# A decoder trunk's prologue rebuilt: half of x first, the activations rounded from the transposes, small loads put off, and one mean-square product a norm

## The chip, the cores and the metric

The kernel runs on one core of a Trainium2 chip. The metric is the device time of one execution in microseconds (us): 1108.33 us is the median of three runs of the kernel before (1108.31 to 1109.08). Five engines work beside each other, each with an instruction stream of its own: TensorE (PE in the rows, with its weight loads PEld), VectorE (DVE), ScalarE (ACT), GpSimd (POOL) and SyncE (SP), which here only issues transfers. They wait for each other on semaphores.

## The reference

A trunk of two layers on x, 256 tokens by 1024 channels, float32. Each layer is

```
x = x + 0.5 * swiglu(rmsnorm(x, g1), w_gate, w_up, w_down)        # width 2816
h = rmsnorm(x, g_mix)
q, k, v, c_b, c_c, c_u, g_attn, g_conv = split(h @ w_in)          # 5120 columns
y_attn = rmsnorm(diff_attention(q, k, v, rel_bias, lam)) @ w_branch_attn
y_conv = (c_b * causal_conv3(c_c * c_u)) @ w_branch_conv
x = x + (sigmoid(g_attn) * y_attn + sigmoid(g_conv) * y_conv) @ w_out
x = x + 0.5 * swiglu(rmsnorm(x, g2), ...)
```

with `rmsnorm(x, g) = x * rsqrt(mean(x*x) + eps) * g`, and `lam = exp(sum(lq1*lk1)) - exp(sum(lq2*lk2)) + const`, one number a layer. The relative-position bias of the attention is a table of 32 buckets by 4 heads, spread over the distances. A last rmsnorm follows.

## The kernel before

**Tiling.** Activations stand transposed, channels on the 128 partitions: `xt` holds x as 8 tiles of 128 channels by 256 tokens. Weights stream in units of 512 KB, 4 tiles of 128 rows by 256 columns (`raw`, a ring of 4 slots). To keep float32 accuracy with the faster rounded format, each operand is split into a rounded part (hi) and the rest (lo). ACT rounds a weight unit (`hi()`, line 474), DVE subtracts it to get the rest (`lo()`, line 755), and PE forms for each of the 4 tiles two products of the hi weights with the 512 columns of hi and lo activations (line 1109) and two of the lo weights with the 256 hi columns (line 1118). One such unit is 16 matmuls. The activations `xm` are split in the same way: gain times x (`xg`), rounded by ACT, subtracted by DVE, in pairs of tiles (`xm_lo` counts finished pairs).

**Units and sets.** Two units with the same 256 output columns make a set, which ends in one of two accumulators `acc`. ACT copies half of it out (`copy_acc`, line 486), DVE adds the other half (`sum_acc`, line 767); only then can PE begin the next set there. In the first two sets behind a norm the units are taken in turn: set 0 first half of x, set 1 first half, set 0 second half, set 1 second half. I number them units 0, 1, 2, 3; later sets take their two units in a row. A gate set and an up set make one pair of tiles of the feed-forward hidden layer (`gate_up`): DVE scales the gate sum by `rstd`, ACT takes Silu, DVE multiplies by the up sum, ACT rounds (line 543), DVE subtracts (line 852). In `gate_up(1)` the units are 7 to 10, `gate_up(2)` begins with unit 11.

**Order within an engine.** Every stream is written out by hand. A weight transfer is issued when the unit four before it has been split by DVE (`lo_split`). ACT's `hi` of a unit waits for the transfer and for PE's end with the unit four before. DVE's `lo` waits for `hi`. PE's `multiply` (line 1098) waits for both before its first matmul.

**The norm.** The mean square over channels is a product with a matrix of 1/1024 (`mean_square`, line 1146): two float32 matmuls over the two halves of `square_sum`. PE does it between units 1 and 2. `norm_start` on DVE (line 800) clears `square_sum` and adds eps, `norm_root` on ACT (line 501) takes the reciprocal root, `norm_rstd` on DVE refines it in three steps. The norm happens six times, and a seventh form at the end uses tokens as columns.

**The prologue.** SP issues both halves of x, then the four first weight units (lines 351 to 358). ACT issues the first norm's gain as a strided load, the bias table and the one-hot `places`. PE turns x by 16 transposes into the accumulators (line 1182). ACT copies them to `xt` (line 565), DVE multiplies by the gain (line 888), ACT rounds (line 572), DVE subtracts (line 903). In between PE spreads the bias table by 8 matmuls (line 1190), ACT copies the four results (line 583). ACT squares x (line 578), DVE sums the squares (line 910). Then ACT sums the lambda products, takes Exp and loads the Silu table again (lines 586 to 597). POOL loads the lambda rows (line 409), multiplies them, issues 14 loads of small parameters (line 419), and sends the bias rows through DRAM and back (lines 431 to 437). PE waits for all four pairs of `xt` before unit 0.

Of the kernel before, what the change touches and what calls it, by code (L numbers as in the profile page):

```python
# [31 lines left out]
P = 128  # L32
# [19 lines left out]
PAIR = 2  # L52
# [3 lines left out]
LEAD = 3  # L56
ACCS = 2
# [41 lines left out]
def bucket_places():  # L99
# [8 lines left out]
    return places  # L108
# [47 lines left out]
def trunk(nc, x, norm_ffn1_g, ffn1_w_gate, ffn1_w_up, ffn1_w_down, norm_mix_g, w_in,  # L156
# [3 lines left out]
    with ExitStack() as ctx:  # L160
# [6 lines left out]
        def sem(name):  # L167
# [28 lines left out]
        square_sum = sb("square_sum", [PAIR, SEQ])  # L196
        mean_sq = sb("mean_sq", [SEQ])
# [28 lines left out]
        first_g = sb("first_g", [KT])  # L226
        eps = sb("eps", [1])
        table_probe = sb("table_probe", [1 + 3 * DEPTH])
# [9 lines left out]
        table_hi = hm[:, 0, :].rearrange("p (h m) -> p h m", h=N_HEADS)  # L238
        table_lo = hm[:, 1, :].rearrange("p (h m) -> p h m", h=N_HEADS)
# [16 lines left out]
        out_msq_ps = acc[0][:, 0, 0:QT]  # L256

# [14 lines left out]
            "x_new", "squared", "square_added", "xg_ready", "xm_hi", "xm_lo"))  # L272
        msq_summed, msq_ready, inv_ready = (sem(n) for n in ("msq_summed", "msq_ready", "inv_ready"))
# [15 lines left out]
            "x_turned", "lam_multiplied", "lam_summed", "lam_exped"))  # L289
        table_ready, bias_spread, bias_rows_ready = sem("table_ready"), sem("bias_spread"), sem("bias_rows_ready")  # L290
# [23 lines left out]
        def _(sp):  # L314
# [21 lines left out]
            def two_sets(l, wa, a, wb, b, in_turn=False):  # L336


                if not in_turn:
                    full(wa, l, a)  # L340
                    full(wb, l, b)
                    return
                for k in range(0, KT, UK):
                    load(rows(wa, l)[:, k:k + UK, bass.ds(a, COLS)])
                    load(rows(wb, l)[:, k:k + UK, bass.ds(b, COLS)])
# [5 lines left out]
            for b in range(2):  # L351
# [3 lines left out]

            for l in range(DEPTH):

                two_sets(l, ffn1_w_gate, 0, ffn1_w_up, 0, in_turn=True)
# [36 lines left out]
        def _(pool):  # L395

            nc.gpsimd.memset(ident[:, :], 0.0).then_inc(ident_zeroed, 1)
            nc.gpsimd.memset(mean_ones[:, :], 1.0 / D_MODEL).then_inc(ones_ready, 1)
# [5 lines left out]
            nc.gpsimd.memset(eps[:, :], SUBLN_EPS).then_inc(ones_ready, 1)  # L404


# [46 lines left out]
        def _(act):  # L453
# [57 lines left out]
            def two_sets(between=None):  # L511
# [3 lines left out]
                if between:  # L515
                    hi()
                    between()
                copy_acc(3 if between else 2)
# [5 lines left out]
            def ffn():  # L524
# [782 lines left out]
```

## Time and profile before

| | us |
|---|---|
| median of three runs | 1108.33 |
| lowest, highest | 1108.31, 1109.08 |
| the profiled execution's own time | 1108.66 |
| its span, first to last instruction | 1106.9 |
| PE busy (share of the span) | 1089.0 (98%) |
| PEld busy | 961.5 (87%) |
| DVE busy | 829.6 (75%) |
| ACT busy | 643.6 (58%) |
| POOL busy | 20.2 (2%) |
| mean traffic of the transfers | 182 GB/s |

The busy times are sums over one engine's instructions; engines overlap, so they do not add up. The outline of the span in 40 slices shows PE at 9 tenths or more in every slice but the first (7) and the last (6). A row of the chain of waits gives start, length and what ran; a row of the timeline gives start, time, engine, line, operation, and in brackets the idle time before it and what ended that.

### The profile page before, as it was taken

How to read it: one execution, taken by the hardware profiler on the slowest of the kernel's cores; microseconds unless marked ns; L12 is line 12 of the kernel's file. 1: busy time of each engine (PE TensorE's matmuls, PEld its weight loads, DVE VectorE, ACT ScalarE, POOL GpSimd, SP SyncE). 2: the span in 40 equal slices, each digit the busy share in tenths (PEclk: the TensorE clock that was granted, in tenths of full speed). 3: DMA queues.
4: the chain of work that ended last, by engine and by line, in shares of the span. 5: the costliest groups of instructions: out<-in, count | busy, mean ns of one | idle time of the engine just before them, and what ended most of it. 6: DMA issues, size and time to landing. Idle time of an engine off the chain costs nothing.

```text
span 1106.9 us, 19503 instructions
## 1 busy us (share of the span) xinstructions
PE 1089.0 (98%) x6512; PEld 961.5 (87%) x6512; DVE 829.6 (75%) x1016; ACT 643.6 (58%) x908; POOL 20.2 (2%) x38
## 2 busy tenths in 40 slices
PE   7999999999999999999999999999999999999996
PEld 6888888888899988888888888888888998888885
DVE  5876766778898877766787776767888988677666
ACT  7655644556775665654466565445767656565454
POOL 5100000000000000000000000000000000000000
PEclk9999999999999999999999999999999999999998
DMA  8856556655566566665566656566455656656561
GB/s 211 250 182 201 175 167 193 203 172 157 170 192 186 163 199 193 180 189 189 178 192 180 202 172 197 168 202 199 145 160 181 200 174 180 200 174 207 169 196 40
DMA packets 202451, 201.64 MB, mean 182 GB/s; under 512 B 7904, under 2 KB 201472, under 8 KB 202416
## 3 DMA queue, kind: packets, MB, share of 16 engines
q1 hardware_dynamic: 200288, 199.25, 58.8%
q0 software_dynamic: 992, 1.87, 0.9%
q8 instruction: 21, 0.34, 0.1%
q10 hardware_dynamic: 1136, 0.05, 0.1%
q14 instruction: 14, 0.11, 0.0%
HBM read 199.32 MB, written 1.84 MB: 182 GB/s over the span
## 4 chain that ended last, share of the span: by engine, by line
PE 97%; DMA 1%; ACT 1%; DVE 0%; issue 0%; SPq 0%; DVEq 0%; ACTq 0%
PE acc L1109 58%; PE acc L1118 31%; PE acc L1113 4%; DMA raw<-in_ffn_w_gate_dram 1%; PE mixed L1113 1%; PE score L1113 1%; PE score L1217 0%; PE mixed L1151 0%; PE mixed L1118 0%; PE score L1118 0%; PE mixed L1238 0%; PE mixed L1225 0%; PE mixed L1231 0%; ACT L508 0%; ACT w_hi L474 0%
## 5 line engine op out<-in xcount | busy, mean ns | idle before, releaser
L1109 PE MATMUL acc<-xm,w_hi 128*128 128x512 f32 x2048 | 648.0, 398 | 2.3 <-ACT xt L565 2.3
L755 DVE TENSOR_TENSOR w_lo<-raw,w_hi 128x1024 fp32r<-128x1024 f32 (+1 forms) x387 | 455.5, 1199 | 139.6 <-ACT w_hi L474 139.2
L1118 PEld LDWEIGHTS acc<-xm,w_lo 128*128 128x128 f32 x2048 | 385.9, 188 | 91.4
L474 ACT CAST w_hi<-raw 128x1024 fp32r<-128x1024 f32 (+1 forms) x387 | 390.5, 1033 | 121.3 <-PE acc L1118 109.6
L1118 PE MATMUL acc<-xm,w_lo 128*128 128x256 f32 x2048 | 403.5, 278 | 0.0
L1109 PEld LDWEIGHTS acc<-xm,w_hi 128*128 128x128 f32 x2048 | 313.4, 189 | 3.1 <-ACT xt L565 2.8
L1109 PE MATMUL acc<-hm,w_hi 128*128 128x512 f32 x704 | 221.1, 395 | 0.0
L1118 PEld LDWEIGHTS acc<-hm,w_lo 128*128 128x128 f32 x896 | 162.2, 189 | 31.3
L1118 PE MATMUL acc<-hm,w_lo 128*128 128x256 f32 x896 | 177.0, 279 | 0.0
L486 ACT COPY acc_lo<-acc 128x512 f32<-128x512 f32 x144 | 84.2, 585 | 128.6 <-PE acc L1118 128.2
L767 DVE TENSOR_TENSOR sum<-acc,acc_lo 128x512 f32<-128x512 f32 x144 | 99.1, 688 | 48.2 <-ACT acc_lo L486 47.4
L1109 PEld LDWEIGHTS acc<-hm,w_hi 128*128 128x128 f32 x704 | 107.2, 189 | 0.0
L543 ACT CAST hm<-ffn_store 128x512 f32 (+1 forms) x44 | 27.4, 622 | 74.2 <-DVE ffn_store L849 74.2
L1113 PE MATMUL acc<-hm,w_hi 128*128 128x256 f32 x384 | 61.7, 283 | 0.0
L852 DVE TENSOR_TENSOR hm<-ffn_store,hm 128x512 f32 (+1 forms) x44 | 30.5, 693 | 33.7 <-ACT hm L543 33.7
L1113 PEld LDWEIGHTS acc<-hm,w_hi 128*128 128x128 f32 x384 | 53.0, 192 | 0.0
L495 ACT ACTIVATE square<-xt 128x512 f32 (+1 forms) x24 | 15.2, 634 | 58.9 <-DVE xt L874 41.3
L536 ACT ACTIVATE ffn_store<-sum 128x512 f32<-128x512 f32 x44 | 27.9, 635 | 29.3 <-DVE sum L837 29.3
L849 DVE TENSOR_TENSOR ffn_store<-sum,ffn_store 128x512 f32<-128x512 f32 x44 | 30.5, 693 | 6.3 <-DVE sum L767 2.5
L837 DVE TENSOR_TENSOR sum<-sum,rstd 128x512 f32<-128x512 f32 x44 | 30.4, 692 | 1.4
L824 DVE TENSOR_TENSOR late<-sum,rstd 128x512 f32 (+1 forms) x28 | 19.4, 692 | 1.0
L945 DVE SCALAR_TENSOR_TENSOR ffn_store<-score,bias 128x768 f32<-128x768 f32 x8 | 7.7, 958 | 16.4 <-PE score L1219 16.4
(145 smaller groups left out, 463.1 us busy)
## 6 DMA issues: line engine op xcount, KB each, us to landing
raw<-in_ffn_w_gate_dram SPq DMA_DIRECT2D x88, 512.0 KB, 4.7
raw<-in_ffn_w_up_dram SPq DMA_DIRECT2D x88, 512.0 KB, 4.0
raw<-in_ffn_w_down_dram SPq DMA_DIRECT2D x80, 512.0 KB, 4.6
raw<-in_w_in_dram SPq DMA_DIRECT2D x80, 512.0 KB, 4.5
raw<-in_w_out_dram SPq DMA_DIRECT2D x16, 512.0 KB, 4.1
raw<-in_ffn_w_down_dram SPq DMA_DIRECT2D x16, 256.0 KB, 3.2
raw<-in_w_branch_attn_dram SPq DMA_DIRECT2D x8, 512.0 KB, 3.5
raw<-in_w_branch_conv_dram SPq DMA_DIRECT2D x8, 512.0 KB, 3.5
```

Of the source, the lines that this page charges most:

```text
L474: nc.scalar.copy(w_hi[:, s, 0:tiles, :], raw[:, s, 0:tiles, :]).then_inc(hi_split, 1)
L486: nc.scalar.copy(acc_lo[s][:, :, :], acc[s][:, :, SEQ:2 * SEQ]).then_inc(acc_copied, 1)
L536: nc.scalar.activation(silu[:, :, :], sums[0][:, :, :], ACT.Silu).then_inc(silu_done, 1)
L543: nc.scalar.copy(hm[:, at(i * PAIR), 0:SEQ], hid[:, :, :]).then_inc(hid_hi, 1)
L755: nc.vector.tensor_tensor(w_lo[:, s, 0:tiles, :], raw[:, s, 0:tiles, :], w_hi[:, s, 0:tiles, :], ALU.subtract).then_inc(lo_split, 1)
L767: nc.vector.tensor_tensor(sums[s][:, :, :], acc[s][:, :, 0:SEQ], acc_lo[s][:, :, :], ALU.add).then_inc(acc_summed, 1)
L837: nc.vector.tensor_tensor(gate, gate, wide(rstd[:, :]), ALU.mult).then_inc(gate_ready, 1)
L849: nc.vector.tensor_tensor(hid[:, :, :], up, silu[:, :, :], ALU.mult).then_inc(hid_ready, 1)
L852: nc.vector.tensor_tensor(h_at[:, :, SEQ:2 * SEQ], hid[:, :, :], h_at[:, :, 0:SEQ], ALU.subtract).then_inc(hid_lo, 1)
L1109: nc.tensor.matmul(banks[:, m, :], w_hi[:, r, k, cols], x[:, 0:2 * SEQ], start=first and k == 0, stop=False, skip_group_check=True)
L1113: nc.tensor.matmul(banks[:, m, 0:SEQ], w_hi[:, r, k, cols], x[:, at_x:at_x + SEQ], start=first and k == 0 and at_x == 0, stop=False, skip_ ...
L1118: mm = nc.tensor.matmul(banks[:, m, 0:SEQ], w_lo[:, r, k, cols], x[:, 0:SEQ], start=False, stop=last and k == ends, skip_group_check=True)
```

## The change

It does five things.

1. **Loads.** SP issues the first half of x, the first gate unit, then the second half of x, then the other units. The first gain is loaded as 8 rows of 128 instead of 1024 single values, and PE transposes it. `places` and the bias table are loaded twice, into 64 partitions. GpSimd's loads wait until the first pair of hidden tiles is rounded (`hid_hi`), and all of its later work stands behind them.
2. **PE.** Eight float32 matmuls of 128 by 128 on the constant matrix run ahead of everything. Only the first half of x is turned before unit 0; the second half is turned behind unit 0. The spreading of the bias table is 4 matmuls over 64 partitions. Unit 0 does all its hi products first and waits for the lo weights only then.
3. **Rounding.** ACT rounds gain times x straight out of the transposes in PSUM, one tile an instruction, and DVE subtracts straight from PSUM too. The copies to `xt` come last on ACT, behind the squares. ACT begins with the Silu table and waits for the small loads (`table_loaded`) before it rounds anything.
4. **Lambdas.** ACT's sums, the Exp and the return to Silu stand behind the second `gate_up` of the first layer.
5. **Norm.** DVE adds the two halves of `square_sum` (`join_squares`), PE does one mean-square matmul instead of two, and does it ahead of unit 3 instead of unit 2. `norm_start` stands behind `sum_acc`, and ACT's root behind `copy_acc`.

```diff
 # SP
-            for b in range(2):
+            def load_x(b):
                 half = slice(b * D_MODEL // 2, (b + 1) * D_MODEL // 2)
                 sp.dma_start(x_tok[:, :, half], ...).then_inc(x_loaded[b], 16)
+            load_x(0)
-                two_sets(l, ffn1_w_gate, 0, ffn1_w_up, 0, in_turn=True)
+                two_sets(l, ffn1_w_gate, 0, ffn1_w_up, 0, in_turn=True,
+                         after_first=None if l else lambda: load_x(1))
 # GpSimd
+            nc.gpsimd.memset(mean_ones[:, :], 1.0 / D_MODEL).then_inc(ones_ready, 1)
+            nc.gpsimd.memset(eps[:, :], SUBLN_EPS).then_inc(ones_ready, 1)
             nc.gpsimd.memset(ident[:, :], 0.0).then_inc(ident_zeroed, 1)
...
+            pool.wait_ge(hid_hi, 1)
             for n, v in enumerate((lambda_q1, lambda_k1, lambda_q2, lambda_k2)):
 # ScalarE
-            act.dma_start(first_g[:, :], columns(norm_ffn1_g[0]), allow_slow_non_contiguous=True) \
+            act.dma_start(gain_rows[0:KT, :], norm_ffn1_g[0].rearrange("(k p) -> k p", p=P)) \
                 .then_inc(gain_loaded, 16)
+            for n in range(2):
+                act.dma_start(table[n * NUM_BUCKETS:(n + 1) * NUM_BUCKETS, :], rel_bias).then_inc(table_loaded, 16)
+            act.dma_start(onehot[0:2 * NUM_BUCKETS, :], places).then_inc(table_loaded, 16)
+            act.wait_ge(ones_ready, 2)
+            have_table(ACT.Silu)
+            act.wait_ge(table_loaded, 48)
+            nc.scalar.copy(onehot_r[0:2 * NUM_BUCKETS, :], onehot[0:2 * NUM_BUCKETS, :]).then_inc(onehot_ready, 1)
+            def pairs_hi(first):
+                for p in (first, first + 1):
+                    act.wait_ge(x_turned, p + 1)
+                    for k in range(PAIR):
+                        last = nc.scalar.activation(xm[:, p * PAIR + k, 0:SEQ], side[p][:, k * SEQ:(k + 1) * SEQ],
+                                                    ACT.Copy, scale=first_g[:, p * PAIR + k:p * PAIR + k + 1])
+                    last.then_inc(xm_hi, 1)
+            act.wait_ge(gain_ready, 1)
+            pairs_hi(0)
+            hi()
             act.wait_ge(bias_spread, 1)
             for h in range(N_HEADS):
-                last = nc.scalar.copy(bias_rows[:, h, :], side[h][:, 0:BIAS_LEN])
+                last = nc.scalar.copy(bias_rows[:, h, :], spread[h][:, 0:BIAS_LEN])
             last.then_inc(bias_copied, 1)
+            hi()
+            pairs_hi(2)
+            hi()
+            for p in range(XPAIRS):
+                act.wait_ge(xm_lo, p + 1)
+                nc.scalar.activation(squares[p]..., side[p], ACT.Square).then_inc(squared, 1)
+            for p in range(XPAIRS):
+                nc.scalar.copy(xt[:, at(p * PAIR), :]..., side[p]).then_inc(x_new, 1)
...
+            def lambdas():
+                act.wait_ge(lam_multiplied, 1)
...
+                have_table(ACT.Silu)
 # ScalarE, gate_up in ffn
-                        norm_root()
-                    copy_acc(3 if first else 2)
+                        wait(act, (square_joined, norm.now + 1))
+                    copy_acc(3 if first else 2)
+                    if first:
+                        norm_root()
...
+                if after_second:
+                    gate_up(1, False)
+                    after_second()
 # VectorE
+            def join_squares():
+                wait(dve, (square_added, pair.now))
+                nc.vector.tensor_tensor(square_one[:, :], square_sum[:, 0, :], square_sum[:, 1, :],
+                                        ALU.add).then_inc(square_joined, 1)
...
                     if first:
-                        norm_start()
                         lo()
                     gate = sum_acc()
                     if first:
+                        norm_start()
                         norm_rstd()
...
+            def pairs_lo(first):
+                for p in (first, first + 1):
+                    dve.wait_ge(xm_hi, p + 1)
+                    for k in range(PAIR):
+                        last = nc.vector.scalar_tensor_tensor(out=xm[:, t, SEQ:2 * SEQ],
+                            in0=side[p][:, k * SEQ:(k + 1) * SEQ], scalar=first_g[:, t:t + 1],
+                            in1=xm[:, t, 0:SEQ].bitcast(F32), op0=ALU.mult, op1=ALU.subtract)
+                    last.then_inc(xm_lo, 1)
+            dve.wait_ge(gain_ready, 1)
+            pairs_lo(0)
+            lo()
+            lo()
+            pairs_lo(2)
+            lo()
 # TensorE
-                wait(pe, (square_added, pairs.now), (bias_copied, 1))
-                for m in range(PAIR):
-                    mm = nc.tensor.matmul(msq_ps, mean_ones[:, :], square_sum[:, m, :], ...)
+                wait(pe, (square_joined, norm.now + 1), (x_new, XPAIRS))
+                nc.tensor.matmul(msq_ps, mean_ones[:, :], square_one[:, :], start=True, stop=True)
...
-                    if between and (j, n) == (0, 1):
+                    if between and (j, n) == (1, 1):
                         between()
+                    if after_first and (j, n) == (0, 0):
+                        multiply_in_two(banks[j], [tiles[:, k, :] for k in range(UK)],
+                                        (made, count.now - UK // PAIR))
+                        after_first()
+                        continue
...
+            pe.wait_ge(ones_ready, 1)
+            for _ in range(WARM):                                        # WARM = 8
+                nc.tensor.matmul(warm_ps, mean_ones[:, :], mean_ones[:, :], start=True, stop=True)
             pe.wait_ge(ident_ready, 1)
+            pe.wait_ge(gain_loaded, 16)
+            nc.tensor.transpose(gain_ps, gain_rows[0:KT, :], ident[0:KT, 0:KT]).then_inc(gain_turned, 1)
+            def second_half():
+                pe.wait_ge(bias_copied, 1)
+                turn_pairs(2)
+            turn_pairs(0)
```

`multiply_in_two` is `multiply` with the 8 hi products first, then the wait for `lo_split`, then the 8 lo products. `turn_pairs` holds the 8 transposes of one half of x.

## Rows read from the trace of the kernel before

**Rows 1.** The page: the chain that ended last, shares of the span by engine

```profile
PE 97%; DMA 1%; ACT 1%; DVE 0%; issue 0%; SPq 0%; DVEq 0%; ACTq 0%
```

**Rows 2.** Chain of waits, first 50 us: start us, length us, what

```profile
1.75 9.97 DMA raw<-in_ffn_w_gate_dram
...
11.74 1.05 ACT w_hi L474
...
19.06 0.85 PE acc L1109 x2
...
21.22 0.46 PE acc L1109 x2
```

**Rows 3.** A window: us, busy us of PE, PEld, DVE, ACT, POOL, PEclk, DMA share, GB/s

```profile
0.00:20.30 20.30, 12.29 (x41) 10.24 (x42) 9.27 (x13) 12.30 (x21) 12.32 (x25) 1.00 0.80 199
```

**Rows 4.** Timeline of PE: start, us, engine, line, operation, count [idle before <-releaser]

```profile
4.91 1.94 PE L1182 MATMUL acc<-ident,late 128*128 128x128 f32 x8 [4.91 <-DMA late<-in_x_dram]
7.16 1.97 PE L1182 MATMUL acc<-ident,late 128*128 128x128 f32 x8 [0.30 <-DMA late<-in_x_dram]
9.64 1.65 PE L1190 MATMUL score<-hm 32*128 32x384 f32 x4 [0.51 <-DVE hm L899]
...
14.85 1.22 PE L1109 MATMUL acc<-xm,w_hi 128*128 128x512 f32 x2 [2.29 <-ACT xt L565]
...
26.84 0.63 PE L1109 MATMUL acc<-xm,w_hi 128*128 128x512 f32 x2
...
38.01 0.63 PE L1109 MATMUL acc<-xm,w_hi 128*128 128x512 f32 x2
```

**Rows 5.** Transfers of the first 12.5 us: issuer, count, KB, us to landing

```profile
part<-in_places_dram ACTq DMA_DIRECT2D x1, 48.0 KB, 6.5
first_g<-in_norm_ffn_g_dram ACTq DMA_DIRECT2D x1, 4.0 KB, 4.6
```

**Rows 6.** Timeline of ACT in the prologue

```profile
8.45 0.51 ACT L569 CAST hm<-part 32x384 fp32r<-32x384 f32 x1 [0.97 <-DMA part<-in_places_dram]
...
18.09 1.15 ACT L578 ACTIVATE acc_lo<-xt 128x512 f32<-128x512 f32 x2
19.14 0.83 ACT L583 COPY proj<-score 128x384 f32<-128x384 f32 x2
...
20.61 0.29 ACT L590 ACTIVATE lam_scratch<-lam_prod 128x64 f32<-128x64 f32 x1
...
21.95 1.28 ACT L508 ACT_TABLE_LOAD   x1
...
23.36 2.94 ACT L474 CAST w_hi<-raw 128x1024 fp32r<-128x1024 f32 x3
```

**Rows 7.** Timeline at the kernel's end: scaled copies out of PSUM, transposes

```profile
1093.87 1.04 PE L1273 MATMUL score<-ident,late 128*128 128x128 f32 x8
...
1101.14 1.57 ACT L725 ACTIVATE late<-score,out_rstd 128x256 f32<-128x256 f32 x4 [0.68 <-DVEq L1077]
```

**Rows 8.** Timeline of DVE: the lo parts of units 3 and 4

```profile
24.42 2.36 DVE L755 TENSOR_TENSOR w_lo<-raw,w_hi 128x1024 fp32r<-128x1024 f32 x2 [1.40 <-ACT w_hi L474]
```

**Rows 9.** Timeline of ACT: the hi parts of units 11 and 12

```profile
44.49 2.00 ACT L474 CAST w_hi<-raw 128x1024 fp32r<-128x1024 f32 x2
```

**Rows 10.** Timeline of POOL

```profile
11.41 0.87 POOL L414 TENSOR_TENSOR lam_prod<-lam_rows 128x128 f32<-128x128 f32 x2 [7.33 <-DMA lam_rows<-in_lambda_k_dram]
...
30.11 0.75 POOL L437 DMA_DIRECT2D bias<-bias_scratch  x1
```

**Rows 11.** Line 862 of DVE: count, duration min/median/max ns, first and last start

```profile
L862 DVE COPY cur<-pars x2: 176/178/179, 144.8 to 683.0; 128x38 f32<-128x38 f32 x2
```

**Rows 12.** Chain of waits at the second norm

```profile
208.17 0.86 PE mixed L1151 x4
```

**Rows 13.** Timeline at the third norm: ACT's hi of units 7, 8; PE's unit 7

```profile
387.19 2.00 ACT L474 CAST w_hi<-raw 128x1024 fp32r<-128x1024 f32 x2
...
391.35 0.63 PE L1109 MATMUL acc<-xm,w_hi 128*128 128x512 f32 x2
```

More of the change, by code:

```diff
@@ L594, in _ @@
[L594 to L599 removed]
+            hi()
+            pairs_hi(2)
+            hi()
+            squares = (square_sum, square, acc_lo[0], acc_lo[1])
+            for p in range(XPAIRS):
+                act.wait_ge(xm_lo, p + 1)
+                nc.scalar.activation(squares[p][:, :, :].rearrange("p k n -> p (k n)"), side[p],
+                                     ACT.Square).then_inc(squared, 1)
@@ new lines, in _ @@
+            for p in range(XPAIRS):
+                nc.scalar.copy(xt[:, at(p * PAIR), :].rearrange("p k n -> p (k n)"), side[p]).then_inc(x_new, 1)
+            pair.add(XPAIRS)
+            def lambdas():
+                act.wait_ge(lam_multiplied, 1)
+                for s in range(2):
+                    for l in range(DEPTH):
+                        n = s * DEPTH + l
+                        last = nc.scalar.activation(lam_scratch[:, s, l * HEAD_DIM:(l + 1) * HEAD_DIM],
+                                                    lam_prod[:, s, l * HEAD_DIM:(l + 1) * HEAD_DIM], ACT.Copy,
+                                                    accum_out=lam_sum[:, n:n + 1])
+                last.then_inc(lam_summed, 1)
+                act.wait_ge(lam_summed, 1)
+                nc.scalar.activation(lam_exp[:, :, :], lam_sum[:, :].rearrange("p (s l) -> p s l", s=2),
+                                     ACT.Exp).then_inc(lam_exped, 1)
+                have_table(ACT.Silu)
@@ L600, in _ @@
+            for l in range(DEPTH):
+                ffn(None if l else lambdas)
                 two_sets(norm_root)
@@ L882, in _ @@
             dve.sem_inc(square_added, 1)
[L884 to L900 removed]
+            dve.sem_inc(xg_ready, XPAIRS)
@@ L1096, in _, with multiply_in_two @@
             slot = [0]
+            def multiply_in_two(banks, x_tiles, *needs):
+                r = slot[0] % RING
+                wait(pe, *needs, (hi_split, unit.now + 1))
+                for k, x in enumerate(x_tiles):
+                    for m in range(PAIR):
+                        nc.tensor.matmul(banks[:, m, :], w_hi[:, r, k, m * P:(m + 1) * P], x[:, 0:2 * SEQ],
+                                         start=k == 0, stop=False, skip_group_check=True)
+                wait(pe, (lo_split, unit.now + 1 + RING))
+                for k, x in enumerate(x_tiles):
+                    for m in range(PAIR):
+                        mm = nc.tensor.matmul(banks[:, m, 0:SEQ], w_lo[:, r, k, m * P:(m + 1) * P], x[:, 0:SEQ],
+                                              start=False, stop=False, skip_group_check=True)
+                mm.then_inc(used, 1)
+                unit.add()
+                slot[0] += 1
             def multiply(banks, x_tiles, first, last, *needs, halves=True):
```

146 lines of the change are left out of this document (59 added, 87 removed).

## The prediction

> **What bounds the kernel now.** I read the page's chain first: 97% of it is PE [rows 1]. So the time is PE's work plus what keeps PE from starting. Then the chain of the first 50 us in order of time: the first gate unit's transfer lands at 11.72 us, ACT rounds it, and the first real matmul starts at 14.85 us [rows 2, 4]. PE waited 4.91 us for x and 2.29 us just ahead of unit 0 [rows 4]. From then on I find no hole in PE: unit 3 starts at 26.84 and unit 7 at 38.01, which makes (38.01 - 26.84) / 4 = 2.79 us a unit [rows 4]. Last the pace: a pair of hi matmuls takes 0.85 us at 19.06 and 0.46 at 21.22 [rows 2]. The granted clock of the window up to 20.3 us reads 1.00 [rows 3], so it misses this; by the pace I take the engine to have run at 1.2 GHz until about 20.3 us and at 2.4 GHz after, though it had turned x and spread the bias table between 4.91 and 12.6 [rows 4].
>
> Two prices follow. A us by which PE's steady run starts earlier is a us of the result, if PE never waits afterwards. And whatever leaves PE's steady stream counts in full. I work out when units 3 and 11 start, where the before has 26.84 and 26.84 + 8 x 2.79 = 49.14.
>
> **When ACT can start.** ACT now rounds nothing before `table_loaded`. The `places` load took 6.5 us from issue to landing, behind the strided gain on the same queue (4.6 us) [rows 5]; ACT found it at 8.45 [rows 6]. It becomes the fourth issue, at about 2.45 us (0.73 + 3 x 0.55, an estimate from the issues' spacing), and twice as large. What goes is the 1024 single values ahead of it and POOL's lambda loads. Bounds: 4.6 us to landing gives 7.05, 6.5 gives 8.95; below, landing stops mattering where the first transposes are done, 4.91 + 1.94 / 2 = 5.9. I take 7.0, the nearest row being the gain's. The gate unit is now second in SP's queue, where the second half of x (same 512 KB) had landed by 7.16 [rows 4], and ACT wants it at 8.95. So that load is hidden. If it still landed at 11.72, all below moves by 2.8.
>
> **ACT up to unit 0.** One-hot copy 0.45 (0.51, ends overlap) [rows 6]; four scaled copies of 256 columns from PSUM, by 1.57 for four at the end of the kernel [rows 7], 1.5; hi(0) 0.98 (2.94 / 3) [rows 6]. 7.0 + 0.45 + 1.5 + 0.98 = 9.95. DVE's share (four fused subtractions, then lo(0)) runs beside it; the split form of unit 0 needs lo(0) only 8 matmuls later. The four spreading matmuls took 1.65 us [rows 4] and fit between 8.1 and 9.8. PE starts unit 0 at 10.0, 4.85 us before the old start.
>
> **The clock.** This is where I must choose. Before, 2.9 us of spreading matmuls and a hole of 2.29 us did not bring the fast level; 5.5 us of unit 0 without a hole did. Now 8 warm-up matmuls of two passes each run from about 1.0 to 4.9 us (16 x 0.24, by the transposes' 1.94 / 8 [rows 4]), then transposes and a wait, then the spreading, a hole of 0.2 to 0.4 us, and unit 0. Bounds: fast from the first matmul, or slow through unit 0 (5.1 us) and, with the transposes interrupting, through unit 1. I take fast from 13.0, some 3 us into unit 0, between the two. Then the hi half of unit 0 ends at 13.25, the lo half (8 x 0.12) at 14.2, four transposes at 0.13 each [rows 7] at 14.7.
>
> **ACT up to unit 3.** The bias copies (1.47 for four, 19.14 to 20.61 [rows 6]) and hi(1) are done by 12.5, hidden under unit 0, and `bias_copied` is there in time. From 14.75: four scaled copies 1.5, hi(2) 1.0, four squares 2.1 (18.09 to 19.14 for two [rows 6]), four copies to `xt` 2.1 (taken as the squares), hi(3) 1.0: 22.45. DVE's lo(3) adds 1.25 [rows 8]: 23.7. PE meanwhile turns the rest of x (done 15.25), runs units 1 and 2 (to about 20.9) and then waits; the mean square, which now needs all of `x_new`, falls into that wait and costs nothing here. So PE holds a hole of some 2.3 us before unit 3. Unit 3 starts at 23.7, which is 3.1 us earlier than before.
>
> **ACT up to unit 11: the lambdas.** Until `gate_up(2)` the chain of ACT and DVE, not PE, sets the pace, as it did before: from hi(3)'s end (23.36 + 0.98 = 24.34) to the end of the second rounding of hidden tiles, where hi(11) starts (44.49), it took 20.15 us [rows 6, 9]. The root now stands behind `copy_acc` and `norm_start` behind `sum_acc`, which I price at 0.5 (0.8 for the two DVE instructions less what waited anyway; bounds 0 and 1.0): 20.65. Then the lambdas. The four sums with Exp took 20.61 to 21.95, 1.34 us, and the Silu table 1.28 [rows 6]. Exp now needs a table of its own, 1.28 more: 3.9 us. Add hi(11) 1.0 and lo(11) 1.25. 22.45 + 20.65 + 3.9 + 2.25 = 49.25. PE would be there at 23.7 + 0.7 (small waits at units 4 and 7) + 8 x 2.79 = 46.7. So PE waits some 2.5 us, and unit 11 starts at 49.25, 0.1 us later than before. The prologue's lead is given back.
>
> ACT must not wait for the lambda rows on top. `hid_hi` comes at about 33.4; the four issues take 2.4 us; before, the product stood ready 7.33 + 0.87 us behind the last issue [rows 10]: 33.4 + 2.4 + 8.2 = 44.0, and ACT arrives at 43.1. In that stretch there is less other traffic, so I take 0, with 0.9 as the bound above by this row.
>
> Later, ACT catches up within one `gate_up`: unit 15 is wanted 11.2 us after unit 11, and a turn of the ACT and DVE chain takes 9.7. POOL's rest (small parameters, bias through DRAM) took 30.86 - 11.41 = 19.5 us [rows 10] and ends near 64, the wait for them on DVE stands at 144.8 [rows 11]. Their traffic beside the weights was there before, at 12 to 36 us, and no weight unit was late.
>
> **The later norms.** One mean square costs PE 0.86 us for the four passes of two matmuls [rows 12]. Half goes: 0.43 in each of the five later norms, 2.15. The root comes later against PE by the one set that it now stands behind. Before, hi(7) began 4.16 us ahead of unit 7 [rows 13] and needs 1.0 + 1.25 with some 0.7 lost to hi(8) and other work between; I reckon hi(7) later by 0.5 and PE earlier by 0.4, which leaves about 1 us. Cost 0, bound 0.4 each. The join is 0.4 us of DVE (estimate, half a 512-column add of 0.69); it lies under units 0 to 2, and at the end under PE's last mean square; bound 0.4 there.
>
> **Sum.** +0.1 (unit 11) - 2.15 = -2.05 us. The profiled execution's own time is 1108.66 for a span of 1106.9; it lies 0.33 above the median. 1106.9 - 2.05 = 1104.85, with 1.76 around it 1106.6, and by the median 1108.33 - 2.05 = 1106.3. I say 1106.3.
>
> **A rule against it.** The table loads follow each other here without a pause: 21.95 + 1.28 = 23.23, and hi(3) starts at 23.36 after the probe [rows 6]. The Trainium skill, ScalarE: Activation LUTs, section What ACT_TABLE_LOAD costs, says that a switch of table costs about 2.66 us, 1.28 for the load and 1.38 of drain. By that rule the two switches of the lambdas would cost 2.8 us more than I count, and the sum would be about 1109.0. The rows show no such drain.
>
> **The rivals.** Everything behind unit 0 hangs on one chain, so a shift of unit 3 is a shift of the result.
>
> *Forecast*, unit 3 near 23.7: 1106.3, own range 1105.3 to 1107.3. Chance 0.40.
>
> *The clock is fast from unit 0 on*: unit 0 takes 2.8, x is turned at 13.3 instead of 14.7, unit 3 starts at 22.3: 1104.9. For it: the warm-ups last 3.9 us and the spreading follows. Against it: the pause between them holds only transposes and waiting, and in the rows transposes with spreading did not do it. An early landing of `places` (5.9) would give up to 1.1 more. Chance 0.26.
>
> *The clock is slow through unit 1*: unit 0 5.1, four transposes 1.0, unit 1 5.1, unit 2 ends at 25.0, mean square, unit 3 at 25.5: 1108.1. Chance 0.10.
>
> *`places` lands late*, at 9.0: the chain moves by 2.0, 1108.3. Chance 0.07.
>
> *The order of loads does nothing*, the gate unit lands at 11.7 still: +2.8, 1109.1. Against it: SP's queue was served in order for x. Chance 0.06.
>
> *The tables drain*, as in the rule above: 1109.1. Chance 0.04.
>
> *Slower: ACT stands at the lambda rows.* ACT's queue is in order; behind the wait stand all hi parts, behind these lo and PE. The rows are fetched through POOL only once `hid_hi` is up, beside the weight stream. Each us by which the product comes after 43.1 is a us of PE idle. It turns the result to a loss from a product at 45.2 (2.05 us late), and beyond the 0.2% from 47.4, that is 11.6 us behind the last issue against the row's 8.2. At 15 us behind it the product comes at 50.8, 7.7 after ACT: 1106.3 + 7.7 = 1114.0. Against it: the row of 7.33 was taken with the transfers at their fullest. Chance 0.07.
>
> **How the numbers follow.** A measurement here tells about 0.2%, 2.2 us, from no change: faster is below 1106.1, slower above 1110.5. Faster: 0.21 of the forecast's 0.40 and all of 0.26, 0.47. Slower: 0.07. Same: 0.46. The range takes the fast clock with part of the early landing (1104.0) and on the other side the late starts (1109.0); it leaves out the slow rival and the tails of the others.
>
> **What would show it.** After: `table_loaded` met near 7.0, first line-1109-like matmul (in the split unit) near 10.0; the pair of hi matmuls falling from 0.85 to 0.46 within unit 0; a PE wait near 2 us before unit 3, released by DVE's lo; a second one near 2.5 us before unit 11, behind an ACT_TABLE_LOAD for Exp; half as many mean-square passes, 12 instead of 24, each saving 0.43; no PE wait at the later norms. The prediction is wrong in its main step if PE shows no wait at unit 11, and then the result is up to 2.5 us better.

## The result, and the profile after

The changed kernel takes 1110.33 us, the median of 17 runs (1108.93 to 1110.82), against 1108.40 for 17 runs of the kernel before beside them (1107.65 to 1109.39). The ratio is 1.0015, with the 95% interval 1.0008 to 1.0021: slower by some 2 us where 2 us less were forecast, above the range's 1109.0. The profiled execution took 1110.61 us for a span of 1108.7; before, it was 1108.66 for 1106.9. So the trace has 1.8 us to explain, and 3.9 against the forecast.

I read it in the order of the prediction. First the page's chain, the row that answers to [rows 1]:

```profile
PE 94%; DVE 2%; ACT 2%; issue 1%; DMA 1%; ACTq 0%; DVEq 0%
```

PE had 97% and now has 94%. The table of waits of PE says for whom it stood (us in total, times, longest):

```profile
PE acc L1172 <- DVE w_lo L785: 4.8, 4, 2.2
PE acc L1268 <- DVE hm L930: 3.5, 1, 3.5
...
PE acc L1243 <- POOL eps L410: 1.0, 1, 1.0
PE acc L1150 <- DVE xm L939: 0.4, 1, 0.4
```

L1172 is the first hi matmul of a unit (L1109 before), L785 is DVE's `lo`. The timeline of PE (start, us, and in brackets the idle time before it) places each, against [rows 4]:

```profile
0.99 3.78 PE L1243 MATMUL acc<-mean_ones 128*128 128x128 f32 x16 [0.99 <-POOL eps L410]
...
5.28 1.10 PE L1255 MATMUL score<-ident,late 128*128 128x128 f32 x8 [0.31 <-DMA late<-in_x_dram]
...
11.95 3.60 PE L1150 MATMUL acc<-xm,w_hi 128*128 128x512 f32 x8 [0.45 <-DVE xm L939]
15.39 1.10 PE L1155 MATMUL acc<-xm,w_lo 128*128 128x256 f32 x8
16.33 1.04 PE L1255 MATMUL mixed<-ident,late 128*128 128x128 f32 x8
...
20.88 0.70 PE L1172 MATMUL acc<-xm,w_hi 128*128 128x512 f32 x2 [0.72 <-DVE w_lo L785]
...
25.72 0.70 PE L1172 MATMUL acc<-xm,w_hi 128*128 128x512 f32 x2 [1.39 <-DVE w_lo L785]
...
37.74 0.70 PE L1172 MATMUL acc<-xm,w_hi 128*128 128x512 f32 x2 [0.45 <-DVE w_lo L785]
...
51.33 0.70 PE L1172 MATMUL acc<-xm,w_hi 128*128 128x512 f32 x2 [2.21 <-DVE w_lo L785]
...
52.79 1.05 PE L1172 MATMUL acc<-xm,w_hi 128*128 128x512 f32 x2
...
54.07 1.05 PE L1172 MATMUL acc<-xm,w_hi 128*128 128x512 f32 x2
```

Unit 0 starts at 11.95, 2.90 us earlier than before, unit 3 at 25.72, 1.12 us earlier, unit 11 at 51.33, where before it stood at 49.16: 2.17 later.

```profile
49.16 0.63 PE L1109 MATMUL acc<-xm,w_hi 128*128 128x512 f32 x2
```

Then, from 52.79 on, hi pairs follow each other by 1.28 us instead of 0.70: the clock. Its granted level stands in the windows (PEclk is the third number from the end, in shares of 2.4 GHz):

```profile
0.00:8.00 8.00, 5.08 (x25) 4.53 (x25) 0.17 (x1) 1.49 (x2) 1.11 (x9) 1.00 0.74 225
8.00:16.00 8.00, 5.69 (x18) 4.49 (x19) 5.12 (x8) 5.43 (x11) 0.00 (x0) 0.57 0.79 245
16.00:20.00 4.00, 4.00 (x29) 3.60 (x27) 2.15 (x5) 3.03 (x7) 0.00 (x0) 1.00 0.46 135
...
52.80:56.50 3.70, 3.70 (x15) 3.12 (x14) 3.17 (x5) 2.15 (x3) 2.97 (x5) 0.54 0.86 260
56.50:60.00 3.50, 3.50 (x22) 3.06 (x22) 2.35 (x4) 1.97 (x3) 0.00 (x0) 1.00 1.02 302
```

The warm-ups did bring the fast level (the 8 transposes take 1.10, against 1.94 before), but PE then had nothing to do: the granted clock falls to the 1.2 GHz level at 8.45 us, in PE's wait of 3.49 us, and is back at about 15.3, some 3.3 us into unit 0. And a second slow stretch, which no step priced, lies just behind the wait at unit 11: PE is busy for all of its 3.70 us, at 0.54 of full speed. By the pace, 52.79 to 56.45 holds three pairs in 3.66 us. At the fast level three pairs take 2.09, so the stretch costs 1.6 us.

What delays unit 11 and unit 0 is on ACT (against [rows 6, 9]):

```profile
8.68 0.51 ACT L584 CAST hm<-part 64x384 fp32r<-64x384 f32 x1 [4.34 <-DMA part<-in_places_dram]
9.09 1.55 ACT L591 ACTIVATE xm<-score,first_g 128x256 fp32r<-128x256 f32 x4
10.53 1.04 ACT L486 CAST w_hi<-raw 128x1024 fp32r<-128x1024 f32 x1
...
44.90 0.25 ACT L619 ACTIVATE lam_scratch<-lam_prod 128x64 f32<-128x64 f32 x1
...
45.98 1.28 ACT L624 ACT_TABLE_LOAD   x1
47.27 0.21 ACT L624 ACTIVATE lam_exp<-lam_sum 128x4 f32<-128x4 f32 x1
47.49 1.28 ACT L520 ACT_TABLE_LOAD   x1
...
48.90 1.98 ACT L486 CAST w_hi<-raw 128x1024 fp32r<-128x1024 f32 x2
```

ACT stood 4.34 us for `places`, and between 44.90 and 48.90 it does nothing but the lambdas. The lambda rows themselves were in time; the timeline of POOL (against [rows 10]) has the product at 42.67, before ACT asks:

```profile
42.67 0.99 POOL L426 TENSOR_TENSOR lam_prod<-lam_rows 128x128 f32<-128x128 f32 x2 [4.64 <-DMA lam_rows<-in_lambda_k_dram]
```

The mean squares are 12 passes where they were 24, the chain of the second norm shows 0.43 us for what was 0.86 [rows 12], and PE waits for no later norm. The balance: unit 11 +2.17, slow clock behind it +1.6, five norms 5 x (-0.43) = -2.15, together +1.6. PE's last transposes, before (first row) and after (second), are 1.68 us apart, which is this sum; the spans differ by 1.8.

```profile
1097.88 0.66 PE L1273 MATMUL mixed<-ident,late 128*128 128x128 f32 x4 [2.53 <-DVE late L792]
1099.56 0.66 PE L1351 MATMUL mixed<-ident,late 128*128 128x128 f32 x4 [2.52 <-DVE late L822]
```

This is the account of one execution. The experiments show that the stretches at 1.2 GHz vary from one profile to the next.

### The profile page after: what moved, and what is told of

The parts are those of the page before. It is cut to its first block, busy times and chain, and to the rows that moved or that the text cites. A ratio compares the mean times of both kernels' runs of the same rounds, so it can differ in the third digit from the quotient of the medians.

```text
span 1108.7 us, 19512 instructions
## 1 busy us (share of the span) xinstructions
PE 1088.9 (98%) x6513; PEld 960.8 (87%) x6513; DVE 830.2 (75%) x1024; ACT 643.0 (58%) x914; POOL 21.0 (2%) x38
## 4 chain that ended last, share of the span: by engine, by line
PE 94%; DVE 2%; ACT 2%; issue 1%; DMA 1%; ACTq 0%; DVEq 0%
PE acc L1172 56%; PE acc L1181 30%; PE acc L1176 4%; PE mixed L1176 1%; PE score L1176 1%; DMA part<-in_places_dram 1%; DVE w_lo L785 0%; PE score L1295 0%; ACT w_hi L486 0%; PE mixed L1181 0%; PE score L1181 0%; PE acc L1150 0%; PE mixed L1316 0%; DVE sum L797 0%; DVE xm L939 0%
## 5 line engine op out<-in xcount | busy, mean ns | idle before, releaser
L1172 PE MATMUL acc<-xm,w_hi 128*128 128x512 f32 x2040 | 644.9, 397 | 4.8 <-DVE w_lo L785 4.8
L785 DVE TENSOR_TENSOR w_lo<-raw,w_hi 128x1024 fp32r<-128x1024 f32 (+1 forms) x387 | 455.3, 1199 | 139.6 <-ACT w_hi L486 139.2
L1172 PEld LDWEIGHTS acc<-xm,w_hi 128*128 128x128 f32 x2040 | 311.6, 189 | 6.0 <-issue 5.6
L1172 PE MATMUL acc<-hm,w_hi 128*128 128x512 f32 x704 | 221.1, 395 | 0.0
L1172 PEld LDWEIGHTS acc<-hm,w_hi 128*128 128x128 f32 x704 | 107.2, 189 | 0.0
```

Of the source, the lines that this page charges most:

```text
L785: nc.vector.tensor_tensor(w_lo[:, s, 0:tiles, :], raw[:, s, 0:tiles, :], w_hi[:, s, 0:tiles, :], ALU.subtract).then_inc(lo_split, 1)
L1172: nc.tensor.matmul(banks[:, m, :], w_hi[:, r, k, cols], x[:, 0:2 * SEQ], start=first and k == 0, stop=False, skip_group_check=True)
```

## The experiments

Each edit is against the changed kernel, unless it says otherwise. In the first four the kernel before took 1108.65 us (33 runs), in the next four 1108.45 (21 runs), in the last two 1108.73 (10 runs). The changed kernel was not run again beside them; a difference to its 1110.33 crosses such groups, between which the kernel before moves by 0.3 us.

**e1_norm_only: the kernel before with part 5 alone.**

```diff
+                join_squares()
...
-                    if between and (j, n) == (0, 1):
+                    if between and (j, n) == (1, 1):
-                for m in range(PAIR):
-                    mm = nc.tensor.matmul(msq_ps, mean_ones[:, :], square_sum[:, m, :], ...)
+                nc.tensor.matmul(msq_ps, mean_ones[:, :], square_one[:, :], start=True, stop=True)
```

> The kernel before with part 5 of the change alone: one mean-square matmul on a joined sum, ahead of unit 3, norm_start behind sum_acc, the root behind copy_acc. Theory (the norm part is sound, the loss is all in the prologue): six norms give 0.43 us each, so 2.6 us less than before, 1105.8 us, and no PE wait at any norm. Rival (the later place of the mean square delays the chain of ACT and DVE so that units 7 and 11 wait): no gain, 1108.4 or a little more, with PE waits behind each norm.

1106.44 us (1105.84 to 1107.09), ratio 0.9982 (0.9973 to 0.9991): -2.2. In the first feed-forward nearly everything is lost to new waits, unit 7 coming only 0.32 us earlier than before, although in this profile PE's pace rises 2.7 us sooner (within the pair at 17.43, before within that at 20.14):

```profile
25.64 0.70 PE L1123 MATMUL acc<-xm,w_hi 128*128 128x512 f32 x2 [0.47 <-DVE w_lo L760]
...
37.69 0.70 PE L1123 MATMUL acc<-xm,w_hi 128*128 128x512 f32 x2 [0.41 <-DVE w_lo L760]
```

Unit 11 stands at 48.91, 0.25 us earlier than before. With the five later norms' 2.15 that makes 2.40, and PE's last transposes do start 2.40 us earlier than before:

```profile
1095.48 0.66 PE L1285 MATMUL mixed<-ident,late 128*128 128x128 f32 x4 [2.52 <-DVE late L797]
```

The spans differ by 2.1: the rest is lost at the very end, where the granted clock has fallen and PE's last matmuls, the mean square of the closing norm, take 1.75 us here and 1.39 before.

So the norm's part is worth what it was priced at, and the other four parts together cost 1110.33 - 1106.44 = 3.9 us.

**e2_lam_late: the lambda block behind the sixth `gate_up` instead of the second.**

```diff
-                    gate_up(1, False)
+                    with loop(act, 6, {...}, 1) as i:
+                        gate_up(i, False)
                     after_second()
```

> The kernel after with ACT's lambda block behind gate_up(5) instead of gate_up(1). Theory: by then ACT is ahead of PE, the 2.2 us wait at unit 11 goes, and the fall of the granted clock at 52.8 us (3.4 us at half speed, 1.65 us lost) goes with it: 1110.3 - 3.9 = 1106.5 us. Rival A (the clock falls there by itself, whatever PE waited for): only 2.2 us, 1108.1. Rival B (the block costs the same wherever it stands): 1110.3.

1108.12 us (1107.97 to 1108.87), ratio 0.9997 (0.9988 to 1.0006): 2.2 us less than the changed kernel, where 3.8 were expected. The block still costs a wait of 0.89 us, so by then ACT's lead covers some 3.1 of its 4.0 us. Behind this shorter wait the granted clock stays at 1.00 in the profile; up to the last transposes the profile is 2.85 us shorter than the changed kernel's, 1.3 of it from the wait and 1.6 from the slow stretch:

```profile
94.64 0.70 PE L1174 MATMUL acc<-xm,w_hi 128*128 128x512 f32 x2 [0.89 <-DVE w_lo L787]
```

**e3_no_warm: no warm-up matmuls.**

```diff
-WARM = 8
+WARM = 0
```

> The kernel after without the eight warm-up matmuls. Theory (they buy nothing, since the granted clock has fallen again at 8.45 us, ahead of unit 0): the transposes are slower by 0.9 us but hidden behind the wait for places; 1110.3 us within 0.8, and unit 0 as slow as with them. Rival (they still shorten the slow stretch of unit 0): unit 0 and part of unit 1 slow, 2 us or more longer, 1112.5.

1110.38 us (1109.86 to 1111.2), ratio 1.0016 (1.0007 to 1.0025): the same as with them. The first transposes are slow again and unit 0 is as slow as with the warm-ups (3.60):

```profile
5.23 1.97 PE L1255 MATMUL score<-ident,late 128*128 128x128 f32 x8 [2.53 <-DMA late<-in_x_dram]
...
12.27 3.75 PE L1150 MATMUL acc<-xm,w_hi 128*128 128x512 f32 x8 [0.48 <-DVE xm L939]
```

In total the warm-ups are worth nothing as the change places them: the fast level that they bring is gone before unit 0. The two profiles reach the same time by different ways, though. Here unit 3 starts later by 1.0 (26.68), since the slow level lasts longer into unit 0 and the transposes behind it. PE waits 2.21 us at unit 11 as in the changed kernel, but the clock does not fall behind that wait, and the 1.6 us come back:

```profile
52.29 0.70 PE L1172 MATMUL acc<-xm,w_hi 128*128 128x512 f32 x2 [2.21 <-DVE w_lo L785]
```

**e4_fill: 16 more dummy matmuls, between the first transposes and the spreading.**

```diff
             turn_pairs(0)
+            for _ in range(16):
+                nc.tensor.matmul(warm_ps, mean_ones[:, :], mean_ones[:, :], start=True, stop=True)
```

> The kernel after with 16 further dummy matmuls between the transposes of the first half of x and the spreading of the bias table, so that PE is busy in the 3.5 us in which it waits for the small loads. Theory: the granted clock stays at 2.4 GHz through unit 0, whose hi half takes 1.9 instead of 3.45 us; unit 3 comes some 1.6 us earlier and the result is 1108.7. Rival (unit 3 hangs on ACT and the late small loads alone): below 0.3 us, 1110.2.

1108.45 us (1107.65 to 1109.83), ratio 1.0001 (0.9992 to 1.001): 1.9 us less than the changed kernel. Unit 0's hi half falls from 3.60 to 2.08 us, and unit 3 comes 1.65 us earlier:

```profile
11.82 2.08 PE L1150 MATMUL acc<-xm,w_hi 128*128 128x512 f32 x8 [0.98 <-DVE xm L939]
...
24.07 0.70 PE L1172 MATMUL acc<-xm,w_hi 128*128 128x512 f32 x2 [1.37 <-DVE w_lo L785]
```

In this profile the granted clock stays at 1.00 in unit 0, and also behind the wait of 2.36 us at unit 11:

```profile
49.83 0.70 PE L1172 MATMUL acc<-xm,w_hi 128*128 128x512 f32 x2 [2.36 <-DVE w_lo L785]
```

Its runs lie in two groups, 1107.65 to 1108.45 at a mean granted clock of 0.996 and 1109.04 to 1109.83 at 0.994 or 0.995. The profile is of the first group. The distance, about 1.5 us, is the price of a fall behind the wait at unit 11, and e7_three and e9_fill_heads, which have the dummies but not this wait, have no run below 0.996. That the second group has such a fall is likely by this, but no profile shows it.

**e5_places_first: `places` is ACT's first transfer.**

```diff
+            act.dma_start(onehot[0:2 * NUM_BUCKETS, :], places).then_inc(table_loaded, 16)
             act.dma_start(gain_rows[0:KT, :], ...).then_inc(gain_loaded, 16)
...
-            act.dma_start(onehot[0:2 * NUM_BUCKETS, :], places).then_inc(table_loaded, 16)
```

> The kernel after with the load of places issued first on ACT's queue instead of fourth (at 0.74 instead of 2.29 us). Theory (ACT's first rounding hangs on this landing, 8.68 us): it lands 1.5 us earlier if it takes its 6.4 us again, the whole chain up to unit 11 moves by 1.5, result 1108.8. Rival (it lands when the traffic of x and the first weights lets it, whatever its place): it lands at 8 us or later, gain under 0.6, 1110.

1110.02 us (1109.37 to 1110.6), ratio 1.0013 (1.0004 to 1.0022): 0.3 less than the changed kernel, no gain to speak of. The gate is met by whichever small load is last, and that is now the bias table, 0.4 us before the old time:

```profile
8.30 0.51 ACT L584 CAST hm<-part 64x384 fp32r<-64x384 f32 x1 [3.80 <-DMA table<-in_rel_bias_dram]
```

Unit 0 starts 0.37 us earlier (11.58), but unit 3 0.92 later (26.64): in this profile the slow level lasts until 17.9 us instead of 15.3, so the lo half of unit 0 takes 1.91 instead of 1.10 (first row). And behind the same wait at unit 11 as in the changed kernel (second row) the clock does not fall:

```profile
15.13 1.91 PE L1155 MATMUL acc<-xm,w_lo 128*128 128x256 f32 x8
52.28 0.70 PE L1172 MATMUL acc<-xm,w_hi 128*128 128x512 f32 x2 [2.22 <-DVE w_lo L785]
```

**e6_lam_heads: the lambda block behind the first head's copies,** where ACT loads the Exp table for the softmax anyway; the lambda parameter is copied apart from the others.

```diff
-                have_table(ACT.Silu)
-                ffn(None if l else lambdas)
+                ffn()
...
                     "p (a h) n -> p h a n", a=3)[:, 0]).then_inc(head_copied, 1)
+                if not l:
+                    lambdas()
```

> The kernel after with the lambda block moved behind the first head_qkv copy, where the Exp table is loaded anyway, so that both extra table loads go. Theory: no PE wait at unit 11 beyond 0.2 us and none elsewhere, and no fall of the granted clock behind it: 1110.3 - 2.2 - 1.3 (the mean of the fall over runs) = 1106.8, which is 1.3 below e2_lam_late, where 0.9 us of waiting was left. Rival (1.3 us of ACT work ahead of the heads delays the first softmax and PE waits there): 1108 or more.

1107.0 us (1106.12 to 1108.97), ratio 0.9988 (0.9979 to 0.9997): -3.3 against the changed kernel. There is no PE wait at unit 11 and no slow stretch behind it. The spread is wide. In the profiled execution, the slowest, unit 3 started at 27.83, 2.1 us later than in the changed kernel. Of these, 1.2 came between unit 0 and unit 1, where the slow level lasted until 18.7 us instead of 15.3; 0.9 came ahead of unit 0 (12.87), for `places` landed later than anywhere else:

```profile
9.59 0.51 ACT L586 CAST hm<-part 64x384 fp32r<-64x384 f32 x1 [5.25 <-DMA part<-in_places_dram]
```

The runs fall into two groups here too: five, among them the profiled one, at a mean granted clock of 0.991 took 1107.90 to 1108.97, six at 0.994 or 0.997 took 1106.12 to 1107.00.

**e7_three: e4, e5 and e6 together.**

> The kernel after with three repairs at once: places first, 16 dummy matmuls behind the first transposes, lambdas behind the first head_qkv copy. Theory (the three losses are separate and add): 1110.3 - 1.5 - 1.6 - 3.5 = 1103.7, and every run within 0.6 of it since no hole of PE over 1.4 us is left. Rival (one of them hides the others, for instance an earlier start makes the units 1 to 3 wait for weights in flight): 1105 or more.

1104.66 us (1104.35 to 1105.28), ratio 0.9964 (0.9950 to 0.9978). The clock's and the lambdas' parts add up (1110.3 - 1.9 - 3.3 = 1105.1). Of the 1.5 us expected of `places` first there is little to see: ACT begins at 8.33, 0.35 us earlier than in the changed kernel.

**e8_double: one more switch to the Exp table and back in the lambda block.**

```diff
                 have_table(ACT.Silu)
+                have_table(ACT.Exp)
+                have_table(ACT.Silu)
```

> The kernel after with one more switch to the Exp table and back behind the lambda block, 2.6 us more of ACT. Theory: PE's wait at unit 11 grows from 2.2 to 4.8 us, one for one, and the granted clock falls behind it in every run: 1110.3 + 2.6 + up to 0.4 = 1113.0 to 1113.4. Rival (ACT has slack there, and the 2.2 us came from elsewhere): less than 1.5 us more.

1115.14 us (1114.26 to 1115.29), ratio 1.0056 (1.0042 to 1.007): +4.8, more than expected. The wait at unit 11 grew by 3.0 us, and the slow stretch with it (windows of us, with PEclk third from the end):

```profile
54.79 1.19 PE L1174 MATMUL acc<-xm,w_hi 128*128 128x512 f32 x2 [5.21 <-DVE w_lo L787]
```

```profile
50.00:55.00 5.00, 0.21 (x1) 0.24 (x2) 1.58 (x2) 4.97 (x8) 5.00 (x7) 0.84 0.29 4
55.00:60.00 5.00, 5.00 (x16) 4.22 (x17) 4.43 (x5) 2.32 (x3) 1.30 (x3) 0.50 0.82 153
60.00:64.00 4.00, 4.00 (x24) 3.52 (x23) 2.08 (x3) 2.06 (x3) 0.00 (x0) 0.97 1.06 401
```

Two table loads of 1.28 us and two probes of 0.2 are the 3.0 us: a table switch in this block is on the path in full. The clock charges the longer wait once more. From unit 11 to unit 15 PE takes 13.70 us, against 12.79 in the changed kernel and 11.23 in e3_no_warm, where it does not fall, so the slow stretch costs 2.5 us here and 1.6 there.

**e9_fill_heads: e4 and e6 together,** the loads in the changed kernel's order.

> The changed kernel with the 16 dummy matmuls behind the first transposes and the lambda block behind the first head's copies; the loads in the order of the changed kernel. Theory (the two edits add up, the order of the small loads is worth nothing): 1110.3 - 1.9 - 3.3 = 1105.1, between 1104.4 and 1105.8; no PE wait at unit 11, none of the clock's falls before it. Rival (the order of loads does matter once the rest is gone, since places landed as late as 9.6 us in one run): about 1106 and a wide spread, unit 3 above 25.

1105.46 us (1104.6 to 1106.21), ratio 0.9969 (0.9957 to 0.9981). 1110.3 - 1.9 - 3.3 makes 1105.1: the two add up. What `places` first adds to them (e7_three) is 0.8 at most, and their runs overlap, so it is not clear of the scatter. ACT begins at 8.80. In this profile the dummies themselves are on the path: they take 4.70 us (3.74 in e4_fill), so by the pace a part of them ran at the slow level, and unit 0 starts with no wait ahead of it. By the changed kernel's 3.27 us from ACT's start to unit 0 it could have started at 12.1:

```profile
7.18 4.70 PE L1269 MATMUL acc<-mean_ones 128*128 128x128 f32 x32
...
12.71 2.11 PE L1154 MATMUL acc<-xm,w_hi 128*128 128x512 f32 x8
```

**e10_no_gate: e9_fill_heads, but ACT rounds x without waiting for the small loads;** 8 dummies instead of 16.

```diff
-            act.wait_ge(table_loaded, 48)
-            nc.scalar.copy(onehot_r[0:2 * NUM_BUCKETS, :], ...).then_inc(onehot_ready, 1)
...
             pairs_hi(0)
             hi()
+            act.wait_ge(table_loaded, 48)
+            nc.scalar.copy(onehot_r[0:2 * NUM_BUCKETS, :], ...).then_inc(onehot_ready, 1)
+            hi()
             act.wait_ge(bias_spread, 1)
...
-            hi()
             pairs_hi(2)
...
 # TensorE, multiply_in_two, behind the 8 hi products
+                spreading()
                 wait(pe, (lo_split, unit.now + 1 + RING))
```

> The same kernel as e9_fill_heads, but ACT no longer waits for the small loads before it rounds x: the one-hot copy stands behind hi(0), hi(1) ahead of the bias copies, DVE's table work behind its first four subtractions, and the spreading between the hi and the lo products of unit 0; 8 dummy matmuls instead of 16. Theory (the wait for places is the term that was missized, everything before unit 3 hangs on it): ACT starts about 6.0 instead of 8.7 us, unit 0 at about 9, unit 3 starts 1.5 to 2.5 us earlier than in e9_fill_heads (22.3 to 23), and the time is 1.7 us lower, about 1103.2. Rival A (the gate hid the gate unit's transfer or the second half of x, which now end last): ACT's hi(0) or the second transposes wait for a transfer and the gain is under 0.7 us. Rival B (the clock: with fewer dummies and an earlier unit 0 the slow level stays on through unit 0, 1.6 us): gain near 0.

1103.74 us (1103.65 to 1103.85), ratio 0.9955 (0.9941 to 0.9969): 1.7 us below e9_fill_heads, as expected, and the fastest here, 5.0 below the kernel before. Its timelines of ACT and of PE:

```profile
6.39 1.57 ACT L590 ACTIVATE xm<-score,first_g 128x256 fp32r<-128x256 f32 x4 [2.05 <-PE score L1258]
...
10.61 1.05 ACT L488 CAST w_hi<-raw 128x1024 fp32r<-128x1024 f32 x1 [1.14 <-DMA raw<-in_ffn_w_up_dram]
12.27 0.86 ACT L602 COPY proj<-acc 128x384 f32<-128x384 f32 x2 [0.61 <-PE mixed L1275]
```

```profile
9.27 2.08 PE L1152 MATMUL acc<-xm,w_hi 128*128 128x512 f32 x8 [0.75 <-DVE xm L932]
...
13.95 1.09 PE L1258 MATMUL mixed<-ident,late 128*128 128x128 f32 x8 [0.57 <-ACT proj L602]
...
23.39 0.70 PE L1175 MATMUL acc<-xm,w_hi 128*128 128x512 f32 x2 [1.37 <-DVE w_lo L787]
```

ACT starts at 6.39, when the first transposes let it, and unit 3 at 23.39 instead of 25.01 in e9_fill_heads. The gain of 2.4 us at ACT's start is 1.6 at unit 3: ACT waits 1.14 us for the first up unit's transfer, and behind it 0.61 for the spreading, which now stands behind unit 0's hi half (L1275). Since this second wait ends later than the transfer, the next limit is the spreading and not the transfer: PE's second transposes wait 0.57 us for the bias copies. PE does not wait at unit 11, which starts at 46.65, 2.5 us earlier than before; with the norms' 2.15 that is 4.7 of the spans' 5.0. The gate and the eight dummies were changed at once: of the 1.6 us at unit 3 some 0.6 are those by which e9_fill_heads's own dummies held up its unit 0 in the profile (12.71 against 12.1). No run removes the gate alone.

## Why the prediction was wrong

The chain from ACT's start to unit 11 was right. The landing of `places` was mis-sized by 1.7 us, a small DVE term was left out, and the slow clock behind the forecast wait at unit 11 stood in the sum with nothing. All three errors go in one direction.

**The load of `places`: 7.0 forecast, 8.68 measured.** This is the first step that failed. I argued that with the strided gain gone it would land as fast as the gain had (4.6 us after its issue); it took 6.4 us, as before (6.5 [rows 5]). The bound of 8.95 in the text had it nearly exactly, and the bound was the row of the load itself, on the same queue: that row should have been the value. What e5_places_first adds is that no single load was to blame, since another small one took its place; what e10_no_gate adds is that the gate was not needed: ACT started at 6.39 without it. Unit 0 came at 11.95 instead of 10.0: 1.7 from the landing and 0.3 from DVE, whose four subtractions were said to run beside ACT. They end at 11.70, behind hi(0), and it is for them that unit 0 waited:

```profile
10.04 1.66 DVE L939 SCALAR_TENSOR_TENSOR xm<-score,first_g,xm 128x256 fp32r<-128x256 f32 x4 [0.23 <-ACT xm L591]
```

**The clock in the prologue: close by luck.** Fast from 13.0 was forecast, some 3 us into unit 0 at 10.0; measured it was about 15.3, some 3.3 us into unit 0 at 11.95. The text took the middle of two bounds and had no mechanism for it. It did not forecast that the warm-ups win the fast level and that the wait for `places` loses it again. In the profiles of e5_places_first and e6_lam_heads the slow level lasted 2.6 to 3.4 us longer. The rival of a fast unit 0 fell, and e4_fill made it true with 16 dummies, for 1.65 us at unit 3 (1.4 had been forecast). The Trainium skill, TensorE: Matmul & The Clock Gate, section HAM oscillation, tells of a kernel in which every wait for a transfer brings the slow level back, and advises to arrange the loop so that PE stays supplied. The traces here agree: the 3.60 us of unit 0's hi half fall to 2.08 once PE is kept busy ahead of it.

**Unit 3: 23.7 forecast, 25.72 measured.** It carries the late start of 1.95 us through. From unit 0 to unit 3 the text has 13.7 us, the trace 13.8; single steps in between are off by up to half a us and cancel.

**Unit 11: 49.25 forecast, 51.33 measured, +0.1 against +2.2.** The same 2 us again, for all hangs on one chain of ACT and DVE, as the text said. The wait itself (2.5 forecast, 2.21 measured) and the price of the lambda block (3.9 forecast; 44.90 to 48.90 is 4.0) were right. The product of the lambdas stood ready at 43.66 (44.0 forecast) before ACT asked for it at 44.90: the rival on the other side did not happen, though the result came out on its side.

**The price of the wait at unit 11: not in the sum.** The text counted the 2.5 us of idleness and nothing behind it. In the trace 3.7 us at 0.54 follow and cost 1.6. The same text had weighed the slow level for the prologue, and did not ask the question of the one other wait of that length which it forecast. The slow stretch is tied to this wait, but not by necessity. No profile without the wait has it (e6_lam_heads, e7_three, e9_fill_heads, e10_no_gate), nor has the one with a wait of 0.89 us (e2_lam_late), and behind the longer wait of e8_double it is longer. Yet of the four profiles with a wait of 2.2 to 2.4 us only the changed kernel's has it.

**The norms: -2.15, right.** e1_norm_only measured -2.2: 2.15 and 0.25 of the first norm up to the last transposes, less 0.3 lost behind them, and no wait came at a later norm.

**The tables: the rule fell.** The Trainium skill, ScalarE: Activation LUTs, section What ACT_TABLE_LOAD costs, has 1.38 us of drain at each switch; here the Exp stands at 47.27, right behind the load from 45.98 that takes 1.28 us, and the next load at 47.49. By that rule the block would have taken 2.8 us more than it did, and no run here shows the drain.

With the measured terms the sum is 2.17 + 1.6 - 2.15 = +1.6, against +1.8 in the spans and +1.9 in the medians. The range was too narrow above because its bounds were taken one at a time, 1108.3 for the late load, while the late load and the slow clock behind the wait came together.

What stays open: why the clock fell behind the wait of 2.21 us in the changed kernel's profile and not behind 2.21 in e3_no_warm's, 2.22 in e5_places_first's and 2.36 in e4_fill's. How many of the changed kernel's 17 runs had this fall is not known either, for their mean clocks (0.991 to 0.994) also hold the slow levels of the prologue and of the kernel's end. The medians of e3_no_warm and e5_places_first are within 0.3 us of the changed kernel's, though their profiles lose in the prologue what its profile loses behind unit 11.

## What to carry to other kernels

Where one chain of engines carries the start, take for a small load beside heavy traffic the row of that load, not that of a quicker neighbour, and do not let such loads gate the first real work: here removing the gate, with fewer dummies, was worth 1.7 us and reordering the loads 0.3 to 0.8, within the scatter of the runs. Price every wait of TensorE that you forecast twice, once as idle time and once as the slow clock that may follow. Keep PE busy up to the real work: warm-ups at the start alone brought nothing, and dummies in the last gap as well brought 1.9 us, but they have to fit into the gap at the slow pace too. An added block on a helper engine costs nothing only where that engine has gathered lead; put a table switch where the table is switched anyway. And do not explain a single profile's us or two without asking where its clock was slow, for this differs between executions of one kernel.

## What the runs showed of the hardware

- Of four profiles with a PE wait of 2.21 to 2.36 us at unit 11, one has a fall of the granted clock behind it, at a cost of 1.6 us. Behind 5.21 us it fell and cost 2.5; behind 0.89 us, and behind the waits of 1.4 us ahead of unit 3, it fell in no profile.
- In the changed kernel's prologue the clock fell in PE's wait for `places` (at 8.45 us) and was back at 15.3 us. With other waits there of 2.1 to 4.3 us it was back at 15.9 (e8_double), 17.9 (e5_places_first) and 18.7 (e6_lam_heads), which moved unit 3 by up to 1.3 us.
- Sixteen passes of 128 columns on constants, ahead of everything, shortened 8 transposes from 1.97 to 1.10 us and the kernel by nothing (1110.38 without them, 1110.33 with them). With sixteen further dummy matmuls in the gap before unit 0 the kernel took 1.9 us less.
- A load of 96 KB issued fourth on its queue beside 1.5 MB of other transfers landed 6.4 us after its issue, and issued first after 5.4 or 5.5 (e7_three, e5_places_first); in one execution, issued fourth, it landed 7.3 us after.
